# Depthwise filter one panel later, last tile stacked from two queues, layer norm chain reordered (one Trainium2 core)

## The reference, cut to what matters

```
def conformer_conv(h, w_pw1, b_pw1, w_dw, b_dw, ln_g, ln_b, w_pw2, b_pw2):
    a, gt = jnp.split(h @ w_pw1 + b_pw1, 2, axis=-1)
    z = a * jax.nn.sigmoid(gt)
    z = depthwise_causal_conv(z, w_dw, taps=31) + b_dw
    z = jax.nn.silu(layernorm(z, ln_g, ln_b))
    return z @ w_pw2 + b_pw2
```

## Time and profile before

| | us |
|---|---|
| median of 3 runs | 1827.83 |
| lowest and highest run | 1827.18, 1831.11 |
| profiled execution, its own time | 1828.5 |
| span of the profiled execution | 1826.7 |
| granted TensorE clock over the span | 0.982 |

### The profile page before, as it was taken

The page is one execution under the profiler, slowest core; times in us unless marked ns, Lnnn a source line. Parts: engine busy times, 40 slices in busy tenths (PEclk is TensorE's granted clock), DMA queues, the critical chain, the costliest instruction groups (busy, mean ns, idle before and its releaser), DMA issues.

```text
span 1826.7 us, 22495 instructions
## 1 busy us (share of the span) xinstructions
PE 1774.2 (97%) x8502; PEld 1433.2 (78%) x8502; DVE 1030.1 (56%) x1257; ACT 661.2 (36%) x768; POOL 184.4 (10%) x128
## 2 busy tenths in 40 slices
PE   7989999999999998899999999999999999999997
PEld 6767788888888765688888888888788888888876
DVE  7667564444444688664444444578856444444465
ACT  5328543333233322443333233342234333323342
POOL 1332100000000246100000000014600000000000
PEclk9899999999999999799999999999999999999998
DMA  6210233333233455133333233332213333323322
GB/s 212 78 46 1 70 92 92 92 104 102 68 97 96 117 147 144 59 96 104 92 92 96 82 96 95 105 86 70 70 61 85 108 92 92 93 85 107 95 86 75
DMA packets 284635, 168.12 MB, mean 92 GB/s; under 512 B 8288, under 2 KB 278528, under 8 KB 284576
## 3 DMA queue, kind: packets, MB, share of 16 engines
q1 hardware_dynamic: 283952, 165.64, 32.2%
q0 software_dynamic: 624, 1.67, 0.3%
HBM read 156.59 MB, written 2.10 MB: 87 GB/s over the span
## 4 chain that ended last, share of the span: by engine, by line
PE 93%; DVE 4%; issue 1%; ACT 1%; DMA 1%; SPq 0%; POOL 0%; DVEq 0%; ACTq 0%; POOLq 0%
PE ps L862 28%; PE ps L864 28%; PE ps L863 28%; PE ps L1192 2%; PE ps L1057 1%; PE ps L1100 1%; PE ps L1082 1%; DMA raw<-in_nsa_w_in_dram 1%; PE ps L1112 0%; PE ps L1300 0%; DVE wlo L1411 0%; DVE act_lo L1441 0%; DVE sqacc L1431 0%; PE ps L934 0%; DVE qkd L1944 0%
## 5 line engine op out<-in xcount | busy, mean ns | idle before, releaser
L862 PE MATMUL ps<-act_hi,whi 128*128 128x512 f32 x1756 | 693.2, 395 | 17.4 <-DVE act_lo L1443 8.7
L863 PE MATMUL ps<-act_lo,whi 128*128 128x512 f32 x1756 | 686.9, 391 | 0.0
L864 PE MATMUL ps<-act_hi,wlo 128*128 128x512 f32 x1756 | 686.7, 391 | 0.0
L1411 DVE TENSOR_TENSOR wlo<-raw,whi 128x2048 fp32r<-128x2048 f32 (+1 forms) x156 | 357.3, 2290 | 183.7 <-ACT whi L542 183.3
L862 PEld LDWEIGHTS ps<-act_hi,whi 128*128 128x128 f32 x1756 | 331.8, 189 | 99.2 <-issue 24.8
L863 PEld LDWEIGHTS ps<-act_lo,whi 128*128 128x128 f32 x1756 | 331.9, 189 | 69.4 <-issue 1.2
L864 PEld LDWEIGHTS ps<-act_hi,wlo 128*128 128x128 f32 x1756 | 331.7, 189 | 69.5
L542 ACT ACTIVATE whi<-raw 128x2048 fp32r<-128x2048 f32 (+1 forms) x164 | 306.6, 1870 | 197.1 <-PE ps L864 185.8
L1425 DVE TENSOR_TENSOR t<-ps,rstd 128x512 f32<-128x512 f32 x151 | 103.6, 688 | 266.0 <-PE ps L864 265.1
L862 PE MATMUL ps<-hid_hi,whi 128*128 128x512 f32 x528 | 208.0, 394 | 0.0
L864 PE MATMUL ps<-hid_hi,wlo 128*128 128x512 f32 x528 | 207.0, 392 | 0.0
(11 more groups left out here) (346 smaller groups left out, 1323.3 us busy)
## 6 DMA issues: line engine op xcount, KB each, us to landing
raw<-in_ffn_w_gate_dram SPq DMA_DIRECT2D x44, 512.0 KB, 3.9
raw<-in_ffn_w_up_dram SPq DMA_DIRECT2D x44, 512.0 KB, 5.1
raw<-in_w_gate_upffn_dram SPq DMA_DIRECT2D x44, 512.0 KB, 4.5
raw<-in_ffn_w_down_dram SPq DMA_DIRECT2D x32, 384.0 KB, 3.7
raw<-in_conv_w_pw_dram SPq DMA_DIRECT2D x24, 512.0 KB, 5.6
raw<-in_w_in_dram SPq DMA_DIRECT2D x24, 512.0 KB, 4.4
raw<-in_ffn_w_down_dram SPq DMA_DIRECT2D x32, 320.0 KB, 4.1
z<-z SPq DMA_DIRECT2D x28, 262.0 KB, 4.9
```

The costliest lines, as they stand in the source:

```text
L862: pe.matmul(out, lhs[0], rhs[0], start=start, stop=False)
L863: pe.matmul(out, lhs[0], rhs[1], start=False, stop=False)
L864: return pe.matmul(out, lhs[1], rhs[0], start=False, stop=stop)
L1411: ve.tensor_tensor(wlo[:, n % 2, a], raw[:, n % 2, a], whi[:, n % 2, a].bitcast(F32), ALU.subtract)\
```

## The change

On PE, convolve(m - 3) stands ahead of panel m for m = 3 to 7, so that three convolutions, 5, 6 and 7, follow the last panel. DVE, ACT and POOL follow: combine(m - 2) within taps(m), with a second one, combine(6), late within taps(7); the cast of zc[0] and the squares one iteration later; POOL's additions one iteration later, with three in the last. The last tile is stacked by two DMAs from SP and two from ACT, and SP's third pw2 load waits for them. In the layer norm PE spreads the mean for DVE first, then the reciprocal, then the mean for ACT; DVE takes the reciprocal ahead of its three subtractions, and ACT the root ahead of the copy.

```diff
+        def shifted(b, i, width):
+            src = z[i * STRIP:(i + 1) * STRIP, b, 0:width]
+            return bass.AP(src.tensor, src.offset, [src.ap[0], [1, NS], src.ap[1]])
 # SP
-                for i in range(NS):
-                    src = z[i * STRIP:(i + 1) * STRIP, b, 0:width]
-                    shifted = bass.AP(src.tensor, src.offset, [src.ap[0], [1, NS], src.ap[1]])
-                    sp.dma_start(z4[:, b, i, 0:width], shifted).then_inc(sem(f"z_stacked{b}"), 16)
+                for i in range(NS if m < KD - 1 else NS // 2):
+                    sp.dma_start(z4[:, b, i, 0:width], shifted(b, i, width)).then_inc(sem(f"z_stacked{b}"), 16)
...
+                if i == 2:
+                    sp.wait_ge(sem(f"z_stacked{(KD - 1) % 2}"), 16 * NS * KD // 2)
                 load(n, n % 2, cols256(t["conv_w_pw2"][0], bass.ds(i * 256, 256), n % 2))
 # POOL
                     pool.wait_ge(sem("ln_pool"), 1)
+                    add_channels(KD - 4, KD - 3)
                     add_channels(KD - 3, 0)
-                if m >= 2:
-                    add_channels(m - 2 if m < KD - 1 else KD - 2, m - 1)
+                    add_channels(KD - 2, KD - 2)
+                elif m >= 3:
+                    add_channels(m - 3, m - 2)
 # ACT
-                if m == 1:
+                if m == 2:
                     act.wait_ge(sem("zc_ready"), 3)
                     cast(z0_hi[:, :], zc[:, 0], "ln_act")
                 if m == KD - 1:
                     act.wait_ge(sem("ln_pe"), 1)
                     act.activation(mean[:, :], bank(T0["pw1"] + 12)[:, :], ACT.Copy).then_inc(sem("ln_act"), 1)
-                    act.wait_ge(sem("ln_pool"), 1)
-                    square(LN, KD - 3, zc[:, 0])
-                if m >= 2:
-                    act.wait_ge(sem("zc_ready"), m + 2)
-                    square(LN, m - 2 if m < KD - 1 else KD - 2, zc[:, m - 1])
+                    b, width = m % 2, S + petaps(m) - NS
+                    act.wait_ge(sem("z_ready"), m + 1)
+                    act.wait_ge(sem("conv_done"), m + 1)
+                    for i in range(NS // 2, NS):
+                        act.dma_start(z4[:, b, i, 0:width], shifted(b, i, width)).then_inc(sem(f"z_stacked{b}"), 16)
+                if m >= 3:
+                    act.wait_ge(sem("zc_ready"), m + 1)
+                    square(LN, m - 3, zc[:, m - 2])
+            act.wait_ge(sem("ln_pool"), 1)
+            square(LN, KD - 3, zc[:, 0])
+            act.wait_ge(sem("zc_ready"), KD + 1)
+            square(LN, KD - 2, zc[:, KD - 2])
             hi(N0["pw2"] + 1)
...
-            act.wait_ge(sem("ln_pe"), 2 + 1)
-            act.activation(mean[:, :], ps[4][:, :], ACT.Copy).then_inc(sem("ln_act"), 1)
             act.wait_ge(sem("ln_dve"), 1 + 1)
             act.activation(tok_rstd, tok_rstd, ACT.Sqrt, bias=eps5[:, :]).then_inc(sem("std_ready"), 1)
             seq.link(act.activation(spare, eps5[:, :], ACT.Silu))
+            act.wait_ge(sem("ln_pe"), 2 + 2)
+            act.activation(mean[:, :], ps[4][:, :], ACT.Copy).then_inc(sem("ln_act"), 1)
+            act.wait_ge(sem("ln_act"), 3)
 # PE
-            for m in range(2, KD):
-                convolve(m - 2)
+            panel2("pw1", 2)
+            for m in range(3, KD):
+                convolve(m - 3)
                 panel2("pw1", m)
...
-            convolve(KD - 2)
-            convolve(KD - 1)
+            for m in range(KD - 3, KD):
+                convolve(m)
...
-            for out in (ps[4], bank(T0["pw1"] + 12)):
+            def spread_mean(out):
...
+            spread_mean(bank(T0["pw1"] + 12))
             repeat_rstd(1, tok_rstd, 7)
+            spread_mean(ps[4])
 # DVE
-                if m:
-                    combine(m - 1)
+                if m >= 2:
+                    combine(m - 2)
                 taps(m, range(middle, late_taps))
                 if m < KD - 1:
                     gate_and_value(m + 1)
                 taps(m, range(late_taps, CONV - 2))
+                if m == KD - 1:
+                    combine(m - 1)
...
-            ve.wait_ge(sem("ln_pe"), 2 + 2)
-            for k in range(2):
+            ve.wait_ge(sem("std_ready"), LN + 1)
+            ve.reciprocal(tok_rstd, tok_rstd).then_inc(sem("tok_inv"), 1)
+            ve.wait_ge(sem("ln_pe"), 2 + 1)
+            for k in range(OWN):
                 ins = ve.tensor_tensor(zc[:, k], zc[:, k], spread[:, :], ALU.subtract)
             seq.link(ins)
-            ve.wait_ge(sem("std_ready"), LN + 1)
-            ve.reciprocal(tok_rstd, tok_rstd).then_inc(sem("tok_inv"), 1)
-            seq.link(ve.tensor_tensor(zc[:, 2], zc[:, 2], spread[:, :], ALU.subtract))
```

## The result

The changed kernel took 1818.72 us in the median of 6 runs (1817.03 to 1821.45), the kernel before 1829.11 in 6 runs beside it. The ratio is 0.9945, interval 0.9933 to 0.9958: about 10 us faster. A second set of the same kernel on another chip gave 0.9957 (0.9944 to 0.9971), about 8 us. The forecast was 1821.5, that is 6.3 faster, with a range from 1817.8 to 1824.3. The measured 1818.72 lies within that range, but outside the forecast's own 1820.0 to 1823.2 and inside that of rival 1 (1818.3 to 1820.0): the gain is larger than forecast. Two executions of all, one of the kernel before (3602 us) and one of run 9 (10125 us), took several times as long and are left out of the ratios.

A forecast was written before the change was run, and what follows sets the result against it. PE was taken to set the pace, busy 97% of the span, with gains only where it waits or its clock drops. Terms -3.9 - 0.2 - 0.8 - 1.4 = -6.3 gave 1821.5 us, range 1817.8 to 1824.3.

The forecast's parts named there:

- rival 1: PE's clock stays up through the shorter pause before the last convolution: 7.8 to 9.5 us faster, 1818.3 to 1820.0; chance 0.24.
- rival 2: Two queues carry the last tile's stack no faster than one: 8.1 as before, 3.8 us faster in all, 1824.0; chance 0.15.
- Step 2, the stack: Stacking tile 7 from two queues takes 6.4, so convolve(7) starts at R + 10.8 against R + 11.0: -0.2 us.
- Step 2, the clock: PE's clock falls late in a pause of 2.6; convolve(7) takes 6.4: -0.8 us, bounds -2.3 and 0.
- Step 3: Layer norm chain in the new order: 6.1 instead of 7.5 from first spread to first silu, -1.4 us.
- step 1: Filter one panel later: 4.79 gained at the start, less one stall of 0.9 before panel 4; R moves by -3.9 us.
- R: Start of the first PE instruction behind panel 7: 721.73 before, forecast at 717.9.
- rival 4: Slower: POOL's new wait for convolve(m - 2) delays its splits, so panels 4 to 7 start late; chance 0.03.
- Rival 3: POOL's split is late at most panels, so step 1 shrinks to nothing: -2.4 to 0, 1825.4 to 1827.8; chance 0.07.

The follow-up runs named there:

- run 9: Changed kernel with a buffer of its own for the last tile's shifted copy, so its stack need not wait for convolution 5; ratio to the kernel before 0.9951.
- run 6: Changed kernel with all four DMAs of the last tile from SP, SP's wait ahead of the third pw2 load kept; ratio to the kernel before 0.9973.
- run 5: Changed kernel, two queues kept, without SP's wait for the last stack ahead of the third pw2 load; ratio to the kernel before 0.9973.
- run 1: The changed kernel again, no edit; ratio to the kernel before 0.9957.
- run 4: Changed kernel with only the later filter: one queue for the last tile, load not held, old norm order; ratio to the kernel before 0.9984.
- Run 10: Changed kernel with ACT's copy of the mean moved behind the first silu and cast, mean spread to another bank; ratio to the kernel before 0.9956.

## Why the prediction was right, and where it was not

The time fell into the stated range because that range had been widened to take in rivals 1 and 2. The forecast's own range missed it by 1.3, and that range was narrower than the bounds of steps 2 and 3 added up with step 1 (1817.2 to 1824.8). In substance, the clock did what rival 1, with a chance of 0.24, said. Against the 9.1 of the stage the sum of 6.3 is 2.8 short, and where it is short is told below, step by step.

**Step 1 held to the tenth.** The forecast of R was 3.9 earlier; it was 3.94 by the stage's own start, and 3.87 to 3.94 in every profile with the later filter. The stall was forecast at 0.9 ahead of panel 4 by walking DVE, ACT and POOL through one period; it was 0.83, released by POOL's split. (Two roundings in that walk, 658.8 for 658.9 and a stall of 0.92 for 0.97, cost nothing.) POOL's new wait for the convolution, in POOL's timeline of the changed kernel:

```profile
669.09 4.64 POOL L461 TENSOR_TENSOR wlo<-raw,whi 128x2048 fp32r<-128x2048 f32 x1
...
683.68 4.60 POOL L461 TENSOR_TENSOR wlo<-raw,whi 128x2048 fp32r<-128x2048 f32 x1
690.23 1.05 POOL L469 TENSOR_TENSOR diag<-par 128x512 f32<-128x512 f32 x1 [1.94 <-PE ps L1207]
696.07 1.30 POOL L449 TENSOR_TENSOR zsum<-zsum,zc 128x512 f32<-128x512 f32 x1 [4.79 <-DVE zc L1858]
```

It waits 1.94 for PE, then 4.79 for DVE's combine, so rival 4 had nearly 5 us in its way. Rival 3 had less: the split of panel 5 ends at 673.73, 1.4 before PE takes the panel (675.14), where 1.8 were forecast. Both fell.

**Step 2, the stack.** "1.1 + 5.2 = 6.3", and then "I take 6.4": it took 6.9 (issue at R + 4.3, start at R + 11.2). The two parts of that sum were both off. I had read SP's four issues as even, one every 1.07, and so had the last one issued 1.1 behind the first. They are not even: in run 6 SP's four take 0.56, 0.60, 1.26 and 1.70, in the changed kernel SP's two take 0.56 and 0.60 and ACT's two 0.66 and 1.66. The last issue thus starts 0.70 behind the first instead of 2.56. But its DMA lands 6.1 after issue and not 5.2. Here are SP's last two issues in run 6, and ACT's last in the changed kernel:

```profile
724.30 1.26 SPq L346 DMA_DIRECT2D z<-z  x1
725.61 1.70 SPq L346 DMA_DIRECT2D z<-z  x1
...
720.96 1.66 ACTq L758 DMA_DIRECT2D z<-z  x1
```

Issue brings 1.9, and the landing takes 1.1 of it back (5.0 for SP's last in run 6, 6.1 for ACT's last here): hence the 0.6 to 0.8 for the second queue. The same term had the hold wrong: I wrote that the third pw2 load "costs nothing", and did not see that holding it pays. Before, SP's own issue of 4.26 had kept the load back; a second queue frees SP and lets the load in, unless it is held, and run 5 is the slowest corner at the start.

So rival 2 was half right. From 721.50 to 726.00 the DMA engines' busy share was 0.95 in the changed kernel, against 0.86 in run 6 while one queue moved the same stack (724.30 to 729.90); yet the second queue still saved 0.6 to 0.8. The Trainium skill, page DMA: Bandwidth & Descriptors, section Issuing engines are not separate DMA queues, says that DMAs share the same 16 DMA engines whichever engine started them, and that starting them from several engines saves only the time to initiate them, usually small beside the DMA. The trace agrees with the sharing (run 5: ACT's DMAs landed after 6.7 instead of 5.7); but the issue is not small here, with 4.25 for four DMAs that each land in about 5 (run 6).

**Step 2, the clock.** "I take it that it falls in 2.6": it did not, in 3.0, so the last convolution took 4.83 and gave -2.32, which was the bound of that term, and not -0.8. This is the step that failed and the mis-sized term that mattered most; what came is the first half of rival 1. Pauses ahead of the last convolution over all runs: in 1.5 (twice), 2.9, 2.9, 3.0 and 3.1 it took 4.83; in 3.7 and 4.0 it took 6.5; in 4.2, 4.7, 6.4, 6.8 and 6.8 it took 7.1 to 7.5. The pause of 2.40 in the earlier trace rows misled me: there the neighbouring work was matmuls of the attention with 64 rows, here it is full strips on both sides. That this is the reason was not tried. The better evidence lay in the very pause that the change shortens: before, the clock had stayed at 1.00 for the first 4.8 of it (the rows under run 1). It would have raised the chance of rival 1, though run 4, with a fall after 2.4, shows that it would have made nothing certain. So part of the 1.5 us beyond the forecast may be owed to the moment at which the pause came; no run here varies that moment alone.

**So the parts do not simply add.** To the start of pw2, from the stage's start, the later filter alone gives 2.5, the queues with the hold 0.4, the norm order 1.9, 4.8 in all; together they give 8.3. Most of the other 3.5 comes from the pause: either measure alone leaves it above 4, both together bring it to 3, in which the clock held, and the last convolution alone is 2.8 shorter than the three singles make it. These are single traces. By the runs' ratios the three singles give 2.9, 2.0 and 2.6, which is 7.5 in all and close to the 8 to 10 of the whole, with intervals over 3 us wide each; the ratios neither show this nor exclude it.

**Step 3.** Forecast -1.4, measured -2.23. I charged two of the three spreads with 2.08, the time of one that stood alone and whose last matmul's end counted. Back to back only the starts count: 1.55 and 1.71 for the first two, and ACT's copy comes 1.39 behind the start of the third, in which the clock was back at its higher level (from 739.4). The order itself was right: the root lies behind the variance, the reciprocal is there at 736.54, before PE begins to spread it (737.13), and silu follows ACT's copy at once. The timelines of DVE and of ACT in the changed kernel:

```profile
735.83 0.16 DVE L1886 SCALAR_TENSOR_TENSOR wtap<-ps,wtap 128x4 f32<-128x4 f32 x1 [0.61 <-PE ps L1223]
736.36 0.18 DVE L1889 RECIPROCAL wtap<-wtap 128x4 f32<-128x4 f32 x1 [0.37 <-ACT wtap L771]
737.38 1.88 DVE L1892 TENSOR_TENSOR zc<-zc,ps 128x512 f32<-128x512 f32 x3 [0.84 <-PE ps L1240]
...
736.03 0.30 ACT L771 ACTIVATE wtap<-wtap,eps 128x4 f32<-128x4 f32 x1 [2.48 <-DVE wtap L1886]
...
740.23 0.60 ACT L774 ACTIVATE mean<-ps 128x512 f32<-128x512 f32 x1 [2.38 <-PE ps L1240]
740.86 0.78 ACT L780 ACTIVATE ps<-t,par 128x512 f32<-128x512 f32 x1
```

ACT waits 2.38 for PE's third spread and then copies: "the copy for POOL is what comes last here" was right too. Run 10 shows that taking it off the path buys little, because the feed of pw2's first panel is next.

**What was left out.** The restart of pw2, of which I wrote "Behind it PE is fed in time and all moves along". It ran its first 48 matmuls in 12.41 instead of 13.22, as the clock came back 3.0 after the start and not 4.8.

## What to carry to other kernels

Where the clock falls in one of PE's pauses, price the pause and the clock together: the microsecond that brought the pause from 4.0 to 3.0 was worth 1.7 more on the matmuls behind it, and two changes that each leave the pause too long can shorten it enough jointly. Look first at when the clock fell within the pause that is there. When part of a transfer goes to a second queue, look at what the first queue does next, and hold back what is not needed soon. A shift of a pipeline by one stage can be priced to the tenth by walking each engine through one period, slack by slack.

## What was not expected of the hardware

The issue of one and the same 264 KB copy does not have one price: in run 6 the four took SP 0.56, 0.60, 1.26 and 1.70, and in the changed kernel the second of ACT took 1.66 while the two of SP took 0.56 and 0.60. A load of 1 MB that started 1.2 us behind the first DMAs of the stack raised the landing of ACT's from 5.7 to 6.7 and its own from 4.0 to 8.3. After PE stopped behind the same kind of convolution, the clock fell after 2.4 in one run and after 4.8 to 5.1 in others. And removing 1.5 of pause (run 9) gave back nothing, since the clock then fell in matmuls of one column that had run at the higher level before; whether the point at which it falls in such a stretch can be steered was not tried.
